# Expert weights read as whole 8 KB rows per partition, with the contraction index renumbered to match

## The reference

```python
def expert_block(args):
    xb, e = args
    return (jax.nn.silu(xb @ w_gate[e]) * (xb @ w_up[e])) @ w_down[e]

y_rows = lax.map(expert_block, (x_rows, block_expert)).reshape(n_rows, d)
```

## Time and profile before

| | |
|---|---|
| median of 3 runs | 3762.75 us |
| lowest, highest | 3755.78, 3776.93 us |
| span of the profiled execution | 3770.2 us |
| time of the profiled execution | the page gives its span alone; it lies 7.45 us above the median and inside the three runs |
| mean granted PE clock | 0.879 |
| first expert phase, from first gather to last blocks | about 2097 to 2610 us |
| second expert phase | about 3173 to 3740 us |
| DMA over the span | 668.33 MB, mean 177 GB/s |

### The profile page before, as it was taken

How to read it: one execution, slowest core, us unless ns; L and a number is a source line. 1 busy time by engine, 2 the same in 40 slices (tenths; PEclk the granted TensorE clock), 3 DMA queues, 4 the chain that set the end, 5 groups by cost and what they waited for, 6 DMA issues and landing times. The chain is left out here.

```text
span 3770.2 us, 42388 instructions
## 1 busy us (share of the span) xinstructions
PE 3199.1 (85%) x14122; PEld 2549.0 (68%) x14122; DVE 2651.3 (70%) x2867; ACT 1395.7 (37%) x1761; POOL 673.3 (18%) x379
## 2 busy tenths in 40 slices
PE   7997899979997899975846699996799864999994
PEld 6766788757765787753735588885576554888883
DVE  4346788654356787576983799997487745999996
ACT  1122111000231111035311577775233522777774
POOL 1002111221002112210621100001233611000001
PEclk9956999989758999988977799998798985999997
DMA  4211455313302555227212799995322216999993
GB/s 147 99 70 62 132 188 184 112 69 123 135 6 78 163 188 176 101 50 171 70 44 98 267 370 367 380 388 218 104 90 70 67 59 221 350 377 383 385 386 142
DMA packets 353278, 668.33 MB, mean 177 GB/s; under 512 B 28576, under 2 KB 145532, under 8 KB 344924
## 3 DMA queue, kind: packets, MB, share of 16 engines
q1 hardware_dynamic: 345852, 643.46, 49.3%
q0 software_dynamic: 7264, 22.82, 1.8%
HBM read 613.04 MB, written 53.18 MB: 177 GB/s over the span
## 5 line engine op out<-in xcount | busy, mean ns | idle before, releaser
L2376 DVE TENSOR_TENSOR expert_w_low<-expert_w_raw,expert_w_high 128x2048 fp32r<-128x2048 f32 x290 | 663.3, 2289 | 84.8 <-ACT expert_w_high L2339 83.4
L2339 ACT CAST expert_w_high<-expert_w_raw 128x2048 fp32r<-128x2048 f32 x290 | 554.6, 1914 | 244.0 <-PE bank L137 178.9
L135 PE MATMUL bank<-first_XH,first_w_high 128*128 128x512 f32 x912 | 365.5, 401 | 26.0 <-DVE first_w_low L207 26.0
L135 PE MATMUL bank<-expert_w_high,expert_x_high 128*128 128x512 f32 x928 | 380.5, 410 | 4.9 <-DVE expert_w_low L2376 4.1
L137 PE MATMUL bank<-expert_w_high,expert_x_low 128*128 128x512 f32 x928 | 365.5, 394 | 0.0
L136 PE MATMUL bank<-expert_w_low,expert_x_high 128*128 128x512 f32 x928 | 363.4, 392 | 0.0
L136 PE MATMUL bank<-first_XL,first_w_high 128*128 128x512 f32 x912 | 360.7, 396 | 0.0
L137 PE MATMUL bank<-first_XH,first_w_low 128*128 128x512 f32 x912 | 360.7, 395 | 0.0
L207 DVE TENSOR_TENSOR first_w_low<-first_w_raw,first_w_high 128x2048 fp32r<-128x2048 f32 (+2 forms) x106 | 313.9, 2962 | 3.6
L205 DVE CAST first_w_high<-first_w_raw 128x2048 fp32r<-128x2048 f32 (+2 forms) x106 | 122.0, 1151 | 197.7 <-PE bank L137 160.6
L2218 POOL DMA_INDIRECT expert_x_rows<-h_rows,slot_token x58 | 68.6, 1184 | 871.5 <-PE bank L2246 859.9
(11 more groups left out here) (477 smaller groups left out, 6769.9 us busy)
## 6 DMA issues: line engine op xcount, KB each, us to landing
expert_w_raw<-in_moe_w_gate_dram SPq DMA_DIRECT2D x116, 1024.0 KB, 7.5
expert_w_raw<-in_moe_w_up_dram SPq DMA_DIRECT2D x116, 1024.0 KB, 12.2
expert_w_raw<-in_moe_w_down_dram SPq DMA_DIRECT2D x58, 1024.0 KB, 13.5
modulation<-in_moe_w_down_dram SPq DMA_DIRECT2D x58, 1024.0 KB, 13.2
ffn_up_mod_w<-in_ada_w_dram SPq DMA_DIRECT2D x48, 1024.0 KB, 5.0
first_w_raw<-in_w_up_dram SPq DMA_DIRECT2D x88, 512.0 KB, 6.8
first_w_raw<-in_w_down_dram SPq DMA_DIRECT2D x22, 1024.0 KB, 4.8
first_w_raw<-in_w_in_dram SPq DMA_DIRECT2D x20, 1024.0 KB, 5.1
```

Source lines behind the costliest of these rows:

```text
L135: nc.tensor.matmul(out, rounded(st[0]), rounded(mv[0]), start=start, stop=False)
L2339: nc.scalar.copy(rounded(high[:, part_of(e, n), :]), weights.place(place)).then_inc(w_high, 1)
L2376: nc.vector.tensor_tensor(rounded(low[:, part_of(e, n), :]), weights.place(place), high[:, part_of(e, n), :], ALU.subtract).then_inc(w_spl ...
```

## The change

Two things change together. A slot's load now gives partition `p` the contraction rows `4p` to `4p+3` of its half (`2p` and `2p+1` for down), which lie side by side in DRAM: 128 runs of 8 KB for a slot instead of 512 of 2 KB or 256 of 4 KB. To match, tile `k` of the turned x must hold contraction rows `4p + k`, so each transpose reads every 4th float of a row (a step of 16 bytes) where it read 128 floats side by side; for the hidden rows it reads every 2nd float (a step of 8 bytes). What is written to PSUM, and all that ACT and DVE do, keeps its shape and its contiguous layout.

```diff
@@ ExpertWeights.load
-        sp.dma_start(self.place(at).rearrange("p (k n) -> p k n", k=tiles),
-                     self.d[name][self.i, bass.ds(e, 1), k0:k0 + tiles * P, :].rearrange("o (k p) n -> p (o k) n", p=P)
+        sp.dma_start(self.place(at), self.d[name][self.i, bass.ds(e, 1), k0:k0 + tiles * P, :].rearrange("o (p k) n -> p (o k n)", k=tiles)
                      ).then_inc(self.loaded[at], 16)
@@ turn_rows
+                rows = xg[par][:, KU * half * P:KU * (half + 1) * P].rearrange("t (p k) -> t k p", k=KU)
                 for k in range(KU):
-                    last = nc.tensor.transpose(ps[X_BANK][:, k * P:(k + 1) * P], xg[par][:, (KU * half + k) * P:(KU * half + k + 1) * P], ident)
+                    last = nc.tensor.transpose(ps[X_BANK][:, k * P:(k + 1) * P], rows[:, k, :], ident)
@@ turn_hidden
+                rows = hid[:, :].rearrange("t (r p k) -> t r p k", r=DOWN, k=KDN)
                 for k in range(D_EXP // P):
-                    last = nc.tensor.transpose(ps[HIDDEN_BANK][:, k * P:(k + 1) * P], hid[:, k * P:(k + 1) * P], ident)
+                    last = nc.tensor.transpose(ps[HIDDEN_BANK][:, k * P:(k + 1) * P], rows[:, k // KDN, k % KDN, :], ident)
```

More of the change, by code:

```diff
@@ L2253, in turn_hidden @@
                     pe.wait_ge(hidden_low, e.at(1, -1))
+                rows = hid[:, :].rearrange("t (r p k) -> t r k p", r=DOWN, k=KDN)
                 for k in range(D_EXP // P):
-                    last = nc.tensor.transpose(ps[HIDDEN_BANK][:, k * P:(k + 1) * P], hid[:, k * P:(k + 1) * P], ident)
+                    last = nc.tensor.transpose(ps[HIDDEN_BANK][:, k * P:(k + 1) * P], rows[:, k // KDN, k % KDN, :], ident)
                 last.then_inc(hidden_turned, 1)
```

## The result

| | before | after |
|---|---|---|
| median, 20 runs each | 3764.14 us | 3777.92 us |
| lowest, highest | 3753.05, 3776.93 us | 3767.00, 3790.76 us |
| ratio, 95% interval | | 1.0033 (1.0022 to 1.0044) |
| span of the profiled execution | 3770.2 us | 3782.3 us |

The change makes the kernel slower by 0.33%, 12.4 us of 3764.14 (8.3 to 16.6; by the two medians it would be 13.8). That is inside the 0.5% that the prediction called no change, but the interval doesn't reach 1: the cost is small and real. The forecast of 3762.0 us is 15.9 us too low; the range to 3818 us holds the result.

What follows compares the result with a forecast made beforehand. The prediction took PE, busy for 360 of 360 us, to bound the expert phase. Its terms summed to 0 + 0 + 0 + 0 = 0, so it forecast the median, 3762 us, with a range of 3750 to 3818 us.

Steps and rivals of the forecast that it cites:

- What bounds the kernel: Expert phase: PE's own instructions fill each block of 17.7 us, and the loads follow with a DMA reserve of 5.4%.
- Loads: Expert weight loads in 8 KB runs: DMA time saved priced at nothing, because PE covers it entirely.
- Rival C: Expert weight loads: DMA becomes the bound through worse-served memory, about +49 us, 3811 us; chance 0.05.
- D: Rival on PE's ordinary matmuls: longer runs relieve contention with DMA writes, so their step shortens, 3733 us; chance 0.07.
- Turning x: 464 transposes of x rows read with a 16-byte step: bounds 0 to +51 us, taken as 0.
- Turning the hidden rows: 232 transposes of hidden rows read with an 8-byte step: bounds 0 to +26 us, taken as 0.
- Rival B: Weight load of the x transposes takes twice as long, +0.11 us each, 3813 us; chance 0.22 (hidden rows too: 3839 us, 0.05).
- The start of each phase: First gather sharing DMA with loads, in each of two layers: -8 to +4 us, taken as 0.
- Coarser packets: Start of each phase: longer packets beside the first gather delay it, worst 1.9 us lost in each layer.
- shorter queues: Start of each phase: shorter DMA queues let the first gather land sooner, best 3.8 us gained in each layer.
- The scatters: POOL's scatters of token numbers before the first gather: from -0.6 us to +5.7 us in a layer.
- The sum: Whole kernel: all terms 0, so no change against the 3770.2 us span; median forecast 3762 us.

Runs made afterwards that it cites:

- e5: The kernel before with every turn's four transposes done four times over into the same place; 3987.28 us, ratio 1.0607 to the kernel before.
- e2: The kernel before with the 8 KB loads alone, transposes still contiguous, second layer's tokens routed otherwise; 3806.52 us, ratio 1.0120 to the kernel before.
- e7: The kernel after with rows already written in tile order by DVE and POOL, so PE reads without a step; 3772.92 us, 1.0022 to the kernel before.
- e4: The kernel before with the change made for gate, up and x alone (step 16 bytes); 3768.30 us, ratio 1.0021 to the kernel before.
- e3: The kernel before with the change made for down loads and hidden rows alone (step 8 bytes); 3766.86 us, ratio 1.0013 to the kernel before.
- e9: The kernel before with SP held until the first two gathers land, ahead of the second block's down loads; 3762.43 us, 1.0003 to the kernel before.
- e1: The kernel before with the stepped transposes of x and hidden rows alone, old loads kept; 3765.69 us, ratio 1.0014 to the kernel before.
- e11: The kernel after with SP held until the first two gathers land, ahead of the second block's down loads; 3768.77 us, 1.0007 to the kernel before.

## Why the prediction was wrong, point by point

**What bounds the kernel** was right. PE fills the expert phase; e5 proves it, where every added transpose lengthened the block by its full 0.109 us (the prediction had 0.11). The long loads, alone in e2 and with unstepped turns in e7, moved a phase of some 500 us by 0.3 us at most and a block of 17.73 us not at all, so "Loads", priced at nothing, was right too, and so was the reason: DMA's share fell and its dry moment grew. Rival C fell with that (0.97 instead of 1.03, no engine waiting for a landing), and so did D (two matmuls in a row start at 2309.40 and 2309.63 us in the kernel after: 0.23 us, as before).

**The step that failed is "Turning x", "I take 0", and "Turning the hidden rows" with it.** The terms are 4.2 and 2.9 us (e4 and e3, turn to turn), 6.7 to 7.1 together, where 0 was taken between bounds of 0 and +51, and 0 and +26. The argument was one of rates: the moving operand reads 2.3 columns for each ns, a transpose's load needs 1.2, so a step has room. It says that the step need not double the time, and it didn't; it can't say that the step costs nothing. With PE full, some 0.01 us on each of 696 transposes must show. The sign that the prediction named went against it: the medians were to keep 139 and 138 ns and came out at 210 and 200. The block was to move by less than 0.3 us and moved by 0.12, which is why the result stays within 0.5%.

**Rival B** named the right place, the weight load of the turned rows, at the wrong size. It took the duration at half clock (231 ns) as twice the step, +0.11 us for a transpose. The load's duration did nearly reach that (210 ns), and yet the step rose by 0.011 only: the duration of a weight load isn't its pace, because loads overlap, with each other and with the matmuls ahead of them (four in 0.67 us, above). B as priced (3813 us) is excluded.

**The rule of the lines.** The Trainium skill, "Advanced Engine Details and Errata", section "Memory Cachelines", would have x (one hit on each 16-byte line) penalised and the hidden rows (two) not. Inside a turn the runs show a cost of 0.011 us for the one and 0.010 for the other, and 0.002 for a step of 32 bytes, which also hits a line only once. For x at 16 bytes the trace agrees that there is a penalty, of a size that the section doesn't give; for the hidden rows and for 32 bytes the measurement differs from the rule, and it decides: two hits on a line were not free, and one hit was nearly so.

**"The start of each phase"**, taken as 0 between -8 and +4, was +2.1 us in the profiled pair, and the controls agree: beside long loads the first gather is used 1.1 us later in layer 1 and 1.3 in layer 2. "Coarser packets" won over "shorter queues". The scatters gave neither of their ends: from the start of the first to that of the last are 10.4 us in layer 1 and 10.5 in layer 2 in both kernels.

**The sum** by these terms would have been 7 + 2 = +9 us, inside the measured 8.3 to 16.6. The remaining 3 to 4 us of the ratio's middle value aren't placed: in the pair they lie in stages that the change doesn't touch and in the granted clock of the first phase's end, and no run here ties them to the change. Packets came to 5358 and not about 4000, because the estimate counted the weight loads alone (4272) and left out the small ones, which were there before.

One detail of the text ahead is to be corrected: it speaks of 29 blocks in each layer, and there are 28 and 30.

## What to carry to other kernels

Where an engine is full for a whole stage, a term taken as 0 because "there is room" needs a measured price, however small: some 10 ns on 696 instructions was more than half of this result. Ask of longer DMA runs who waits for a landing: here nobody did inside the phase, so they made the queues lighter for nothing, and they delayed the one small transfer that was waited for. And to measure an effect of 0.2% in a kernel whose runs scatter by 0.6%, enlarge it (the turns four times over), or read it in the trace: a block's length, which was the same to about 0.01 us in every kernel with the same turns and order (17.73 in before, e2, e7 and e9; 17.85 in after, e1 and e11), or a phase from the first to the last start of one group, which repeated to 0.6 us between kernels with the same turns (before, e2, e7 and e9 in layer 1; before, e7 and e9 in layer 2), where the medians scattered by several.

## What the runs showed of the hardware that was not expected

- A weight load (128 x 128, float32) read with a step of 8 or 16 bytes shows 200 and 210 ns instead of 139, and costs PE 0.010 and 0.011 us more from one transpose to the next inside a turn. With 32 bytes it shows 189 ns and costs 0.002. The cost doesn't grow with the step. Why is open; no run here tests it.
- What a step costs isn't all inside the turn: with the hidden rows' step alone (e3) a block is 0.07 us longer, of which 0.03 lie in the turn. What makes up the rest is open.
- A gather of 128 rows of 4 KB is used after 4.7 us with no weight loads beside it, 7.9 and 6.7 us beside down loads in runs of 4 KB, and 9.0 and 8.0 beside down loads in runs of 8 KB.
- A DVE multiply of 128 x 512 that writes every second float takes 1101 ns instead of 680.
